# First block's attention: narrow value products spread over three steps, one modulation slot a step later, and constants' products inside the joints' sums

## The reference, cut to what matters

```python
def diff_attention(q, k, v, lam):            # first block; 4 heads, two softmaxes per head
    ...
        p = jax.nn.softmax(s, axis=-1)
        a = p[:, :, 0] - lam * p[:, :, 1]
        return jnp.einsum('bhqk,bkhe->bqhe', a.astype(v.dtype), v)

def ada_chunks(cvec, w, b):                  # second block: the modulation, needed only later
    m = jax.nn.silu(cvec) @ w + b
    return jnp.split(m[..., None, :], 6, axis=-1)

# second block, between two of its stages
h = h + gt_m * rms_norm_2(y, g_post_m)
f = conv_ffn(modulate(h, g_pre_f, sh_f, sc_f), w_up[layer], conv_w[layer], conv_b[layer], w_down[layer])
```

## Time and profile before

| | |
|---|---|
| device time, 3 runs | 1686.56, 1686.87, 1688.16 us, median 1686.87 |
| profiled execution, its own time | 1687.93 us |
| its span | 1686.1 us |
| TensorE busy | 1619.8 us (96%) |
| VectorE busy | 1019.0 us (60%) |
| ScalarE busy | 870.1 us (52%) |
| mean granted TensorE clock | 0.993 |

### The profile page before, as it was taken

How to read it: one execution, slowest core, us unless ns; L and a number is a source line. 1 busy time by engine, 2 the same in 40 slices (tenths; PEclk the granted TensorE clock), 3 DMA queues, 4 the chain that set the end, 5 groups by cost and what they waited for, 6 DMA issues and landing times.

```text
span 1686.1 us, 28193 instructions
## 1 busy us (share of the span) xinstructions
PE 1619.8 (96%) x11870; PEld 1408.8 (84%) x11870; DVE 1019.0 (60%) x1577; ACT 870.1 (52%) x1467; POOL 21.0 (1%) x38
## 2 busy tenths in 40 slices
PE   6999999999999999999989999999999899999997
PEld 6968999989779999987758777888888675789997
DVE  7675545465856565724465764425555777687685
ACT  6764434457545444534565553323444557766563
POOL 0000000000000000310000000000000000000000
PEclk9999999999999999999999999999999999999999
DMA  7365445354546464772201552232213530154642
GB/s 298 139 239 220 163 154 200 130 197 149 201 173 253 142 237 140 220 237 75 75 2 67 183 200 101 77 134 101 84 53 126 196 129 26 60 216 158 230 150 88
DMA packets 60524, 253.94 MB, mean 151 GB/s; under 512 B 4976, under 2 KB 8304, under 8 KB 42480
## 3 DMA queue, kind: packets, MB, share of 16 engines
q1 hardware_dynamic: 59088, 249.01, 41.5%
q0 software_dynamic: 1312, 3.15, 1.0%
HBM read 251.09 MB, written 1.05 MB: 150 GB/s over the span
## 4 chain that ended last, share of the span: by engine, by line
PE 82%; DVE 10%; ACT 6%; issue 2%; DMA 0%; SPq 0%; DVEq 0%; ACTq 0%
PE PA L925 63%; PE PA L985 3%; DVE W_t L1580 2%; PE PB L860 2%; PE PA L1013 2%; PE PB L1348 2%; ACT W_t L2306 1%; PE PB L1335 1%; PE PA L962 1%; PE PA L967 1%; PE PA L961 1%; PE PA L880 1%; PE PB L1278 1%; DVE Y L1962 1%; PE PA L1420 1%
## 5 line engine op out<-in xcount | busy, mean ns | idle before, releaser
L925 PE MATMUL PA<-XH_t,W_t 128*128 128x256 f32 (+2 forms) x3968 | 873.4, 314 | 4.1 <-DVE W_t L1580 1.8
L925 PEld LDWEIGHTS PA<-XH_t,W_t 128*128 128x128 f32 x3968 | 650.6, 188 | 59.8 <-issue 6.0
L1580 DVE TENSOR_TENSOR W_t<-raw,W_t 128x1024 fp32r<-128x1024 f32 (+1 forms) x344 | 445.1, 1299 | 306.1 <-ACT W_t L2306 305.5
L925 PE MATMUL PA<-XL_t,W_t 128*128 128x256 f32 (+2 forms) x1984 | 620.7, 313 | 0.0
L2306 ACT ACTIVATE W_t<-raw 128x1024 fp32r<-128x1024 f32 (+1 forms) x344 | 381.5, 1113 | 158.4 <-PE PA L925 136.8
L925 PEld LDWEIGHTS PA<-XL_t,W_t 128*128 128x128 f32 x1984 | 373.0, 188 | 23.2 <-issue 0.5
L925 PE MATMUL PA<-AH_t,W_t 128*128 128x256 f32 (+2 forms) x1232 | 266.6, 311 | 0.2
L925 PEld LDWEIGHTS PA<-AH_t,W_t 128*128 128x128 f32 x1232 | 201.6, 188 | 14.1 <-DVE AL_t L1626 0.8
L925 PE MATMUL PA<-AL_t,W_t 128*128 128x256 f32 (+2 forms) x616 | 191.1, 310 | 0.0
L2464 ACT ACTIVATE tmp<-PA,par 128x512 f32<-128x512 f32 (+1 forms) x88 | 58.5, 668 | 132.9 <-PE PA L925 125.2
L1703 DVE SCALAR_TENSOR_TENSOR tmp<-PA,par,tmp 128x510 f32<-128x510 f32 (+1 forms) x88 | 53.7, 614 | 120.4 <-ACT tmp L2464 119.5
(11 more groups left out here) (275 smaller groups left out, 1577.2 us busy)
## 6 DMA issues: line engine op xcount, KB each, us to landing
raw<-in_w_ada SPq DMA_DIRECT2D x48, 1024.0 KB, 4.9
raw<-in_w_gu SPq DMA_DIRECT2D x44, 1024.0 KB, 4.8
raw<-in_w_dn SPq DMA_DIRECT2D x64, 704.0 KB, 4.0
raw<-in_w_up SPq DMA_DIRECT2D x44, 1024.0 KB, 4.8
raw<-in_w_in SPq DMA_DIRECT2D x30, 1024.0 KB, 5.8
raw<-in_w_out SPq DMA_DIRECT2D x12, 1024.0 KB, 4.8
raw<-in_w_qkv SPq DMA_DIRECT2D x6, 1024.0 KB, 6.3
raw<-in_w_outc SPq DMA_DIRECT2D x4, 1024.0 KB, 4.8
```

What stands on the lines that cost most here:

```text
L925: mm = pe.matmul(PA[:, (L.b0 + o) % 4, 0:T], W[:, c:c + P], X[:, k, L.x0:L.x0 + T], start=(n == 0 and m == 0 and not L.early), stop=(n == ...
L1580: dve.tensor_tensor(WL_t[:, w:w + L.cols], RAWV[:, r % RAW, part * UNIT:part * UNIT + L.cols], WHf[:, w:w + L.cols], ALU.subtract).then_in ...
```

## The change

Three edits, all in TensorE's list:

```diff
@@ joint_pe
                 pe.wait_ge(S("j_d"), J.d0 + KD)
                 add(last, 0, 1, False, True).then_inc(S("j_sum"), 1)
+                keep_busy(PA[:, 0, :], 3)
 
                 pe.wait_ge(S("j_c"), J.c0 + KD)
                 pe.wait_ge(S("j_b"), J.b0 + KD)
@@ mix1_pe
                     turn(u)
-                    if u in (2, 3):
-                        values(0, range(2 * u - 4, 2 * u - 2))
+                    if u == 1:
+                        values(0, (0, 1))
+                    elif u == 3:
+                        values(0, (3,))
                     elif u in (4, 6):
                         values(u // 2 - 1)
                     if u == 3:
                         ada_turn()
-                    if u in (0, 1, 4, 5, 6, 7):
-                        n = 2 + u - 2 * (u >= 4)
+                    if u in (0, 2, 4, 5, 6, 7):
+                        n = (u + 4) // 2 if u < 4 else u
                         ada_sums(A.first + n, A.raw0 + n)
+                    if u == 2:
+                        values(0, (2,))
                 values(4)
```

## The result

| | before | after |
|---|---|---|
| device time, 19 runs each | 1685.27 to 1691.94, median 1688.16 us | 1688.78 to 1694.04, median 1691.68 us |
| ratio | | 1.0018 (95% interval 1.0010 to 1.0025) |
| profiled execution, own time | 1687.93 us | 1689.18 us |
| its span | 1686.1 us | 1687.4 us |
| step 0's transpose to `values(4)`, layers 0 and 1 | 21.02, 22.51 us | 23.24, 23.36 us |

The account below looks back on a forecast made before the run. TensorE's list and clock were taken as the bound. Terms -1.54 - 2.93 + 0.3 + 0.3 + 0.1 + 0.8 - 0.5 gave -3.5 against 1687.93, so 1684.5 us; 8-in-10 range 1683.0 to 1687.4.

Parts of the forecast that it names:

- What bounds the kernel: Whole kernel: TensorE, busy 96% of the span; time is won only where it works faster or stops waiting.
- three places: Granted clock at 1.2 GHz in layer 0's attention (3.4 us), layer 1's (6.8 us) and the second joint (3.4 us).
- I take it that the clock then holds: Attention: with narrow groups spread over steps 1, 2 and 3 and wide work between most, the clock stays full.
- the terms -1.54 and -2.93: Attention: gains in us from full clock, 1.54 in layer 0 and 2.93 in layer 1.
- One sign that was named for a right forecast: Layer 0's attention: scores of unit 6, at 110.98 us before, would take 0.70 us.
- The waits, +0.3 a layer: Attention: TensorE waits for ScalarE's copy, and unit 4's scores come later; +0.3 us per layer, between 0.1 and 0.8.
- The joints: Six added constants' records: first joint +0.1, second -0.5 as its clock holds, third +0.8 us from delayed sums.
- Rival 4: Joints: the added constants cost nothing, giving 1683.6 us; chance 0.10.
- Slot A7's late load: Attention: A7's load starts near 108.7 us instead of 106; priced at nothing, at most 2.7 us.
- Rival 3: Attention: clock falls a step earlier and stays low over two stretches in both layers, 1691.9 us; chance 0.04.
- Rival 2: Attention: only gaps lower the clock, so the new order gains nothing there, 1688.9 us; chance 0.06.
- The range: Whole kernel: 8-in-10 range 1683.0 to 1687.4 us; forecast's own range 1683.4 to 1685.8, chance 0.54.

Follow-up runs that it names:

- experiment 3: Kernel before with each of the 24 narrow records streaming 128 columns instead of 16, ScalarE's copy split in two: 1685.57 us, ratio 0.9984 against before.
- experiment 1: Kernel after without the constants' products in the joints, so the attention's edit alone: 1691.68 us, ratio 1.0023 against the kernel before.
- experiment 4: Attention order of the kernel after, no constants in the joints, narrow records widened to 128 columns: 1687.12 us, ratio 0.9996 against the kernel before.
- experiment 2: Kernel before with only the constants' products added in the three joints: 1687.19 us, ratio 1.0001 against the kernel before.
- experiment 8: Kernel before with the last sixteen queries' values turned round, attention weights stationary and v streaming 128 columns, old places: 1682.48 us, ratio 0.9966 against before.
- experiment 9: experiment 8 plus the constants' products in the second joint only: 1682.22 us, ratio 0.9966 against the kernel before.

## Why the prediction was wrong, point by point

**What bounds the kernel**: right. TensorE's list and its clock made every difference in the study, and a narrow record's time was read rightly: in the profile before, the twelve weight loads of the first narrow group take as long as its twelve matmuls.

```profile
106.65 1.71 PEld L1278 LDWEIGHTS PB<-tmp 128*128 128x128 f32 x12
```

Two readings were off without harm. Of the 32 records between 107 and 111 us, 23 have 16 columns and not 18. And low speed is not confined to three places: at the start of the kernel records of 272 columns took 1.11 us for four until about 22 us and 0.66 us behind that, although the granted clock is given as 1.00 throughout. Why, no run tells.

**"I take it that the clock then holds"**: this is the step that failed, and with it the terms -1.54 and -2.93. The sizes were right; experiment 3 recovers the clock and comes to the very attention times that they imply. But spreading the narrow records didn't recover it: in experiment 1 the mean clock fell by 0.0017 instead, which is about 5.7 us more at 1.2 GHz in an execution, and at 1.5 us for each 3.4 us (layer 0's stretch) about 2.5 us of time. That is an estimate; it agrees with experiments 1, 3 and 4, where the new places cost 3.8 us with narrow records and 1.55 with wide ones, so 2.2 for the narrowness. In the sum a term of -4.5 thus stands where the runs have about +2.

I had argued from the two groups of 12 and the little work between them, and asked only whether the new groups stood apart. I didn't count what stands around the first of them on its new step: ahead of it a slot, short scores and one short transpose; behind it short scores and a transpose. In the profile after, the clock fell there; in experiment 1's, with the same list, it fell in slot A3 behind it. The second fall came behind the six and six, where TensorE had also waited 0.32 us for VectorE; experiment 4 has a like wait at that place (0.83 us between the starts instead of 0.63) with wide records, and its clock stayed at 1.00. The runs with 16, 64 and 128 columns at one order show that the width of the moving side counts. What they don't show is why the new places are worse than the old on the mean, and that stays open. That the thin work simply fills a longer piece of the loop, from step 1 to step 4 instead of from 2 to 4, would fit, but was not tried alone.

One sign that was named for a right forecast came with the wrong one: the scores of unit 6 take 0.70 us at 111.13, and the clock falls directly behind them.

**The waits, +0.3 a layer**: the mechanism right, the size 0.58 by the profiles of experiments 3 and 4, within the bounds of 0.1 to 0.8 (0.8 a layer by their medians). The copy's 0.2 came as forecast. VectorE's wait at unit 4, which I had put only into the upper bound, was there.

**The joints**: +0.1, -0.5 and +0.8 were forecast; +0.02, -0.69 and +0.82 came in the profiles. The sum of +0.4 reads as +0.15 there and as nothing in the runs of experiment 2. By the eight profiles without the constants the second joint is at the low clock in six, at a price of 0.7 to 1.3 us, 0.8 on the mean of all eight, and that is just what the third joint loses. Rival 4 (the constants cost nothing) falls by the third joint. VectorE's timeline after has a wait of 0.75 us for the last sums there:

```profile
1478.88 0.23 DVE L1839 TENSOR_TENSOR tmp<-PB,tmp 128x64 f32<-128x64 f32 x1 [0.75 <-PE PB L1030]
```

**Slot A7's late load**: nothing, as said; no row of slot A7 in the profile after has a wait for a transfer.

**The rivals.** Rival 3 came: a fall one step earlier, two low stretches in each layer, 1691.9 us by its sum and 1691.68 measured. That the sum is so near is partly luck: it left out the second joint's gain, had 0.6 for waits that came to 1.2, and set out from 1687.93, which seemed to lie 1.06 above the median and lies 0.2 below that of the 19 runs. It was given 0.04, and what spoke against it, that slot A3's wide records come right behind, was the same unexamined step as in the forecast. Rival 2, that only gaps lower the clock, falls with experiment 3. Between 106 and 111 us TensorE was busy for 5.00 of 5.00 us there; in the kernel before it was as busy in the same window:

```profile
106.00:111.00 5.00, 5.00 (x39) 4.14 (x39) 3.93 (x18) 3.07 (x13) 0.00 (x0) 1.00 1.00 350
```

Behind the one the clock stayed, behind the other it fell. The Trainium skill, TensorE: Matmul & The Clock Gate, in the part on HAM oscillation, makes idle gaps the cause. This trace doesn't agree for narrow records. For the fall in experiment 8, behind waits of 0.17 and 0.42 us, the runs leave it open, since the same waits passed without a fall in experiment 9.

**The range.** It was built around one profile and three runs. The 19 runs of before alone spread over 6.7 us, more than the whole range of 4.4. The times I had, with a step of about one low stretch between them, said as much, and I used them only to place the profile. The forecast's own lower edge was also 0.4 too low: with the bounds as given (0.2 less in each layer's waits, 0.2 in the joints) it is 1683.8 and not 1683.4.

## What to carry to other kernels

Where TensorE is busy all the time and its clock still falls, look at how many columns its records stream: here products whose moving side is 16 columns wide cost their weights' load and, in many executions, the clock of what follows. The one spreading of such work that was tried made it worse; what helped was to turn the product round, or to stream more columns, so that none is narrow. And where the low clock comes and goes between executions, one profile gives the price of a low stretch but not how many there will be: take the mean clock of many runs.

## What the runs showed of the hardware that was not expected

- The same kernel has its low stretches in different number from one execution to the next: mean clocks of 0.990 to 0.995 over the 19 runs after. Across those runs the time was about 0.9 us longer for each 0.001 that the mean clock was lower. The places differ too: with the same instructions and waits, experiment 8's profile has a fall in layer 0's attention and experiment 9's has none.
- Twelve float32 records with 128-column weights took 1.70 us with 16 moving columns, 1.86 with 64 and 2.08 with 128. The weights' load does not hide the columns entirely.
- With 32-column weights in four column groups, 24 records of 128 columns took 0.99 us, less than 12 narrow ones with full weights.
